# Three of eight weighted expert ranks added by TensorE through diagonals, in a two-block network on one core

## The chip, the core and the metric

The kernel runs on one core of one Trainium2 chip. A core has five engines that matter here: TensorE (matmuls into PSUM, the accumulators), VectorE, ScalarE, GpSimd (POOL in the profile) and SyncE (SP), whose queue only issues transfers. They meet through semaphores. The metric is the device time of one execution in microseconds (us), lower is better; the figure of a kernel is the median of its runs.

## What is computed

Two transformer-like blocks on 512 tokens of width 1024, in float32. The first block ends with a mixture of experts: every token picks 8 of 64 experts, each expert gives it one row of 1024 numbers, and the eight rows are weighted and added, together with a shared expert's output. Of the reference this is the part that matters:

```python
wts = jnp.take_along_axis(scores, top_e, axis=1)
wts = wts / jnp.sum(wts, axis=-1, keepdims=True) * ROUTED_SCALE
...
def expert_block(args):
    tok_b, w_b, e = args
    xb = h[tok_b]
    hid = jax.nn.silu(xb @ w_e_gate[e]) * (xb @ w_e_up[e])
    return (hid @ w_e_down[e]) * w_b[:, None].astype(h.dtype)
...
routed = jax.ops.segment_sum(out.reshape(n_pad, d), buf_tok, num_segments=n_tok)
shared = (jax.nn.silu(h @ w_sh_gate) * (h @ w_sh_up)) @ w_sh_down
return routed + shared
```

After it: `x = x + gt2 * rmsnorm(f_lat, g_post_ffn)`, then the second block.

## The kernel before

Everything of a width of 1024 is held feature-major: 8 tiles of 128 features by 512 tokens. The program is a list of stages (`phases`); each engine runs its function of a stage and all compute engines then meet (`meet`, L3059 to L3061). SP is outside of that: it has one stream of its own, which issues in program order, and a transfer that must wait holds everything behind it in the stream.

The experts' rows are unweighted when the expert stage (`moe_*`) writes them to `ys` in device memory, at row `k * T + token` for rank k (the k-th of a token's eight experts). The **gather stage** follows. Tokens go in four tiles of 128 (`TT` = 4), and for tile t and rank k one transfer (a gather, number n = 8t + k) brings 128 rows of 1024 numbers, 512 KB, into buffer `GB[k]`; there are eight buffers, so gather n goes where gather n - 8 was. In this stage

- SP issues the 32 gathers (L1817 to L1821), then the next chunks of the weight stream (`ring`, L3092), which the second block's first projection reads;
- VectorE (`gather_vector`) multiplies each arrived rank by its column of weights `W8[:, t, k]` and adds it up in `H2TOK[:, t, :]` (tokens by features), in the order of the ranks; each operation counts up `g_used`, and SP waits on that count before it refills a buffer;
- TensorE (`gather_tensor`) first puts the shared expert's second matmul into all eight PSUM banks (L2045), then, for each finished token tile, adds `H2TOK` on top: a matmul with the identity as moving operand turns tokens by features into features by tokens while it adds (L2050);
- ScalarE (`gather_scalar`) copies the eight banks out at the end (L2057).

The line by which SP holds a gather back:

```python
if n >= 8:
    sp.wait_ge(sem("g_used"), n - 7)
```

Behind the gather stage stand two norms (`norm`), each a chain ScalarE, VectorE, TensorE, ScalarE, VectorE, and then the projections of the second block (`dil_*`), where ScalarE takes the first weight chunk out of the ring at L259. DVE in the profile is VectorE, ACT is ScalarE. An f32 matmul leaves two records of a matmul and two of a weight load.

Of the kernel before, what the change touches and what calls it, by code (L numbers as in the profile page):

```python
# [16 lines left out]
ACT = mybir.ActivationFunctionType  # L17
# [7 lines left out]
P = 128  # L25
D = 1024
KT = D // P
# [3 lines left out]
TT = T // P  # L31
# [91 lines left out]
def two_blocks(nc, wstream, x_t, ctx_t, vecs, consts, rope_t, gmask_t, dmask_t, iota_t, w_dt, w_router,  # L123
               we_gu, we_down, w_z, w_gate_fb, h2, ys, x_saved, out_t, dbg, stop):
    ctx = ExitStack()
    with ctx:
# [5 lines left out]
        def sem(name):  # L132

            if name in MOE_SEMS:
                name = BLOCK1_SEMS[6 + MOE_SEMS.index(name)]
            if name in BLOCK2_SEMS:
                name = BLOCK1_SEMS[BLOCK2_SEMS.index(name)]
            if name not in made:
                made[name] = ctx.enter_context(nc.semaphore(name))
            return made[name]  # L140
# [26 lines left out]
        def bank(b, n=512, off=0):  # L167
            return pf[:, b * 512 + off:b * 512 + off + n]

        def view(at, *dims):  # L170
            n = 1
            for d in dims:
                n *= d
            ap = arena[:, at:at + n]
            if len(dims) == 2:
                return ap.rearrange("p (a b) -> p a b", b=dims[1])
            if len(dims) == 3:
                return ap.rearrange("p (a b c) -> p a b c", b=dims[1], c=dims[2])
            return ap
# [18 lines left out]
        C = {name: cst[:, i, :] for i, name in enumerate(CONSTS)}  # L198
        XT = view(0, KT, T)
        HT = view(4096, KT, T)  # L200
        R = 8192
# [24 lines left out]
        def arrived(pe, c):  # L226
            pe.wait_ge(sem(f"slot{c % NSLOT}_full"), 16 * (c // NSLOT + 1))
# [5 lines left out]
        def chunk_done(ins):  # L233
            ins.then_inc(sem("chunk_done"), 1)
# [1307 lines left out]
        H2TOK = view(R, TT, D)  # L1542
# [12 lines left out]
        W8 = view(K0, TT, 8)  # L1555
# [225 lines left out]
        def pairs(eng):  # L1781
            return eng.value_load(NPI[0:1, 0:1], min_val=T * 8 // P // 2, max_val=MAXBLK // 2)

        def moe_sync(sp):
            def load_gate_up(s, e):
                for j in range(2):
                    sp.dma_start(arena[:, EW[s][j]:EW[s][j] + CHW], we_gu[bass.ds(e * 2 + j, 1)].rearrange("o p n -> (o p) n")
                                 ).then_inc(sem(f"moe_w{s}{j}"), 16)

            def load_down(s, e):  # L1790
                sp.dma_start(arena[:, EW[s][2]:EW[s][2] + CHW], we_down[bass.ds(e, 1)].rearrange("o p n -> (o p) n")
                             ).then_inc(sem(f"moe_w{s}2"), 16)

            sp.wait_ge(sem("h2_tok"), 8)
            sp.dma_start(h2.rearrange("(t p) d -> p t d", p=P), H2TOK).then_inc(sem("h2_stored"), 16)
            sp.wait_ge(sem("rt_blocks"), 1)
            first = [sp.value_load(BEI[0:1, s:s + 1], min_val=0, max_val=E_N - 1) for s in range(2)]
            for s in range(2):
                load_gate_up(s, first[s])
            for s in range(2):  # L1800
                load_down(s, first[s])
            sp.wait_ge(sem("stage_ended"), 4 * MOE_STAGE)
            n = pairs(sp)
            with sp.Fori(1, n) as i:
                for s in range(2):
                    e = sp.value_load(BEI[0:1, bass.ds(i * 2 + s, 1)], min_val=0, max_val=E_N - 1)
                    for j in range(2):
                        sp.wait_ge(sem("moe_gu_used"), i * 4 + (2 * s + j + 1))
                        sp.dma_start(arena[:, EW[s][j]:EW[s][j] + CHW],
                                     we_gu[bass.ds(e * 2 + j, 1)].rearrange("o p n -> (o p) n")).then_inc(sem(f"moe_w{s}{j}"), 16)  # L1810
                for s in range(2):
                    e = sp.value_load(BEI[0:1, bass.ds(i * 2 + s, 1)], min_val=0, max_val=E_N - 1)
                    sp.wait_ge(sem("moe_d_used"), i * 2 + (s + 1))
                    load_down(s, e)
            for s in range(2):
                sp.wait_ge(sem(f"moe_out{s}"), n * 16 + 16)
            for n in range(32):  # L1817
                t, k = divmod(n, 8)
                if n >= 8:
                    sp.wait_ge(sem("g_used"), n - 7)  # L1820
                sp.dma_start(GB[n % 8], ys[k * T + t * P:k * T + t * P + P, :]).then_inc(sem(f"gathered{n % 8}"), 16)  # L1821

        def expert_hi(s, j):
# [202 lines left out]
        GB = [view(R + 6144 + 1024 * i, D) for i in range(8)]  # L2026
        F = view(R + 14336, KT, T)

        def gather_vector(dve):
            for n in range(32):  # L2030
                t, k = divmod(n, 8)
                dve.wait_ge(sem(f"gathered{n % 8}"), 16 * (n // 8 + 1))
                if k == 0:
                    dve.tensor_scalar(H2TOK[:, t, :], GB[n % 8], W8[:, t, 0:1], None, ALU.mult).then_inc(sem("g_used"), 1)
                else:
                    dve.wait_ge(sem("g_used"), n)
                    dve.scalar_tensor_tensor(H2TOK[:, t, :], GB[n % 8], W8[:, t, k:k + 1], H2TOK[:, t, :], ALU.mult,
                                             ALU.add).then_inc(sem("g_used"), 1)

        def gather_tensor(pe):  # L2040
            c = CH_SH + 2
            arrived(pe, c)
            for j in range(KT):
                for k in range(2):
                    pe.matmul(bank(j), ring[:, c % NSLOT, k * D + j * P:k * D + j * P + P], SHID[:, k, :],  # L2045
                              start=(k == 0), stop=(k == 1))
            for t in range(TT):
                pe.wait_ge(sem("g_used"), 8 * t + 8)
                for j in range(KT):
                    mm = pe.matmul(bank(j, P, t * P), H2TOK[:, t, j * P:j * P + P], C["ident"], start=False,  # L2050
                                   stop=(t == TT - 1), skip_group_check=True)
            chunk_done(mm)

        def gather_scalar(act):
            act.wait_ge(sem("chunk_done"), CH_SH + 3)
            for j in range(KT):
                act.activation(F[:, j, :], bank(j), ACT.Copy)  # L2057

        phases.append(dict(tensor=gather_tensor, scalar=gather_scalar, vector=gather_vector))
        norm(F, T, None, lambda k: gain[:, G2 + k:G2 + k + 1], residual=XT)  # L2060

# [1016 lines left out]
        def _(sp):  # L3078
            first_sync(sp)
            for c in range(CH_END if stop is None else LIMIT):  # L3080
                if c == CH_SH + 3:
                    moe_sync(sp)
                last = c - NSLOT
                if last in SPLIT and run_of(last) in LO_APART:
                    sp.wait_ge(sem("chunk_lo"), SPLIT.index(last) + 1)
                elif last >= 0:
                    sp.wait_ge(sem("chunk_done"), last + 1)
                if last == CH_DIL - 1:
                    sp.wait_ge(sem("semaphores_cleared"), 1)
                if last == CH_DIL:  # L3090
                    dil_swap(sp, 0)
                sp.dma_start(ring[:, c % NSLOT, :], wstream[c]).then_inc(sem(f"slot{c % NSLOT}_full"), 16)  # L3092
                if c == CH_ADA + NSLOT - 1:
                    tokens_sync(sp)
                if c == CH_QKV - 1:
                    tables_sync(sp)
                if CH_QKV <= last < CH_QKV + 8:
                    qk_swap(sp, last - CH_QKV)
                if CH_DIL <= last < CH_DIL + 35:
                    dil_swap(sp, 2 * (last - CH_DIL) + 1)  # L3100
                    dil_swap(sp, 2 * (last - CH_DIL) + 2)
# [29 lines left out]
def program(nc, a, out_t, dbg=None, stop=None):  # L3131
    h2 = nc.dram_tensor("h2", (T, D), F32, kind="Internal").ap()
    ys = nc.dram_tensor("ys", (8 * T + 1, D), F32, kind="Internal").ap()
    x_saved = nc.dram_tensor("x_saved", (P, KT, T), F32, kind="Internal").ap()
    two_blocks(nc, a["wstream"], a["x_t"], a["ctx_t"], a["vecs"], a["consts"], a["rope_t"], a["gmask_t"],
               a["dmask_t"], a["iota_t"], a["w_dt"], a["w_router"], a["we_gu"], a["we_down"], a["w_z"],
               a["w_gate_fb"], h2, ys, x_saved, out_t, dbg, stop)
# [129 lines left out]
```

## Time and profile before

| | us |
|---|---|
| median of 3 runs | 3883.09 |
| lowest, highest | 3882.57, 3893.02 |
| the profiled execution | 3883.08 |
| its span in the profile | 3881.3 |
| TensorE matmul busy in the span | 3554.1 (92%) |
| VectorE busy | 1576.2 (41%) |
| ScalarE busy | 1413.9 (36%) |

The span is what the hardware profiler recorded; what lies around it is start and end of the execution. The gather stage is a short stretch of it, from 1842.6 to 1897 us. A share of busy time over the whole span mixes all stages, so for one stage the timeline (instructions in order of time, neighbours of one line merged) and the windows (busy time in a given stretch) are the views to read. All times in the timeline count from the span's start.

### The profile page before, as it was taken

What the parts mean: (1) busy time and instruction counts of PE and PEld (TensorE: products, weight loads), DVE (VectorE), ACT (ScalarE), POOL (GpSimd) and SP (SyncE); (2) the same over time, 40 slices, a digit from 0 to 9 for tenths busy, and PEclk for the clock granted to TensorE, in tenths of its full rate; (3) what the DMA queues carried; (4) which work ended last, traced back from release to release, by engine and by line L of the source; (5) the groups of instructions that cost most, each with busy time, mean ns of one, the idle gap of its engine ahead of it and who ended that gap; (6) DMA issues with size and microseconds to landing.
All of it is one profiled execution on the core that took longest, in us unless ns stands there. A gap on an engine that the chain in (4) does not pass through costs nothing.

```text
span 3881.3 us, 44158 instructions
## 1 busy us (share of the span) xinstructions
PE 3554.1 (92%) x17320; PEld 2729.8 (70%) x17320; DVE 1576.2 (41%) x2226; ACT 1413.9 (36%) x1738; POOL 1189.7 (31%) x555
## 2 busy tenths in 40 slices
PE   7999897799869999999378999999999998899999
PEld 5975586578636766666257777776788877678887
DVE  4146525620266666665632333334421231243212
ACT  4135433342235555554133343443322232133221
POOL 3410123634202333332033323331344432124443
PEclk9999998899979999999589999999999997589999
DMA  5312110022229999997622221221222211013222
GB/s 217 94 66 88 64 56 22 1 76 98 87 95 335 354 349 355 368 367 287 238 65 87 71 74 60 74 71 49 88 98 98 98 55 55 1 55 109 98 98 76
DMA packets 94478, 494.53 MB, mean 127 GB/s; under 512 B 21646, under 2 KB 21902, under 8 KB 43760
## 3 DMA queue, kind: packets, MB, share of 16 engines
q1 hardware_dynamic: 74496, 452.75, 32.6%
q0 software_dynamic: 19824, 39.54, 2.8%
q8 instruction: 116, 1.90, 0.2%
q14 instruction: 42, 0.34, 0.0%
HBM read 470.18 MB, written 40.89 MB: 132 GB/s over the span
## 4 chain that ended last, share of the span: by engine, by line
PE 45%; DVE 2%; ACT 1%; issue 1%; POOL 1%; POOLq 0%; DMA 0%; ACTq 0%; DVEq 0%
PE ps L272 10%; PE ps L273 10%; PE ps L274 10%; PE ps L2219 2%; PE ps L2196 2%; PE ps L2174 1%; PE ps L2186 1%; PE ps L2207 1%; PE ps L2175 1%; PE ps L2176 1%; PE ps L2845 1%; PE ps L2832 1%; PE ps L2198 1%; PE ps L2840 0%; PE ps L280 0%
## 5 line engine op out<-in xcount | busy, mean ns | idle before, releaser
L272 PE MATMUL ps<-arena_r,arena_r 128*128 128x512 f32 x2080 | 844.1, 406 | 39.7 <-POOL ring_r L263 25.0
L273 PE MATMUL ps<-arena_r,arena_r 128*128 128x512 f32 x2080 | 817.7, 393 | 0.0
L263 POOL TENSOR_TENSOR ring_r<-ring,arena_r 128x2048 fp32r<-128x2048 f32 x100 | 466.2, 4663 | 887.7 <-ACT arena_r L259 887.7
L259 ACT ACTIVATE arena_r<-ring 128x2048 fp32r<-128x2048 f32 x166 | 316.7, 1909 | 564.0 <-PE ps L274 409.8
L272 PEld LDWEIGHTS ps<-arena_r,arena_r 128*128 128x128 f32 x2080 | 394.8, 190 | 144.7 <-issue 52.6
L273 PEld LDWEIGHTS ps<-arena_r,arena_r 128*128 128x128 f32 x2080 | 395.4, 190 | 88.5 <-issue 10.8
L263 POOL TENSOR_TENSOR arena_r<-ring,arena_r 128x2048 fp32r<-128x2048 f32 x66 | 303.9, 4605 | 414.4 <-ACT arena_r L259 414.4
L274 PE MATMUL ps<-arena_r,arena_r 128*128 128x512 f32 x1056 | 411.1, 389 | 0.0
L274 PE MATMUL ps<-arena_r,ring_r 128*128 128x512 f32 x1024 | 406.1, 397 | 0.0
L1949 DVE TENSOR_TENSOR arena_r<-arena,arena_r 128x2048 fp32r<-128x2048 f32 x132 | 301.8, 2288 | 165.2 <-ACT arena_r L1907 165.0
L1907 ACT ACTIVATE arena_r<-arena 128x2048 fp32r<-128x2048 f32 x132 | 250.8, 1910 | 124.6 <-DMA arena<-we_gu 101.3
L278 PE MATMUL ps<-arena_r,arena_r 128*128 128x256 f32 (+2 forms) x784 | 253.5, 323 | 15.5 <-DVE arena_r L300 15.5
L1861 PE MATMUL ps<-arena 128*128 128x512 f32 x528 | 240.7, 599 | 5.6 <-ACT arena L1924 5.1
L1846 PE MATMUL ps<-arena_r,arena_r 128*128 128x512 f32 x528 | 222.5, 421 | 5.2 <-DVE arena_r L1954 5.2
L274 PEld LDWEIGHTS ps<-arena_r,arena_r 128*128 128x128 f32 x1056 | 198.3, 188 | 41.1
L274 PEld LDWEIGHTS ps<-arena_r,ring_r 128*128 128x128 f32 x1024 | 196.6, 192 | 42.4
L1850 PE MATMUL ps<-arena_r,arena_r 128*128 128x512 f32 x528 | 207.0, 392 | 0.0
L1849 PE MATMUL ps<-arena_r,arena_r 128*128 128x512 f32 x528 | 206.5, 391 | 0.0
L2347 DVE CUSTOM_DVE_ANT_0 ps<-ps,arena 128x768 f32<-128x768 f32 x64 | 61.9, 967 | 298.8 <-PE ps L2198 298.8
L2600 DVE TENSOR_TENSOR arena<-ps,arena 128x512 f32<-128x512 f32 x44 | 30.4, 692 | 363.8 <-PE ps L274 363.8
L2313 POOL TENSOR_TENSOR arena<-arena,rope 128x512 f32<-128x512 f32 x48 | 62.0, 1291 | 373.3 <-DVE arena L2330 373.3
L278 PEld LDWEIGHTS ps<-arena_r,arena_r 128*128 128x128 f32 (+1 forms) x784 | 149.9, 191 | 28.7 <-issue 13.4
(388 smaller groups left out, 6101.1 us busy)
## 6 DMA issues: line engine op xcount, KB each, us to landing
ring<-wstream SPq DMA_DIRECT2D x193, 1024.0 KB, 4.9
arena<-we_gu SPq DMA_DIRECT2D x132, 1024.0 KB, 7.9
arena<-we_down SPq DMA_DIRECT2D x66, 1024.0 KB, 7.5
arena<-ys SPq DMA_DIRECT2D x32, 512.0 KB, 8.5
arena<-arena SPq DMA_DIRECT2D x192, 64.0 KB, 2.0
arena<-arena SPq DMA_DIRECT2D x32, 128.0 KB, 4.2
arena<-x_t SPq DMA_DIRECT2D x1, 2048.0 KB, 15.8
h<-arena SPq DMA_DIRECT2D x1, 2048.0 KB, 6.6
```

The source lines that it names most:

```text
L259: act.activation(whalf(c, 0), ring[:, c % NSLOT, :], ACT.Copy).then_inc(sem("chunk_hi"), 1)
L263: pool.tensor_tensor(whalf(c, 1), ring[:, c % NSLOT, :], whalf(c, 0).bitcast(F32), ALU.subtract).then_inc(sem("chunk_lo"), 1)
L272: pe.matmul(out, hi, rhs[0], start=start, stop=False)
L273: pe.matmul(out, hi, rhs[1], start=False, stop=False)
L274: return pe.matmul(out, lo, rhs[0], start=False, stop=stop)
L278: pe.matmul(out, a[0], b[0], start=start, stop=False)
L1846: mm = pe.matmul(bank(4 + s), x[0], hi[:, q * 512:q * 512 + 512], start=(k == 0), stop=False)
L1849: pe.matmul(bank(4 + s), x[0], lo[:, q * 512:q * 512 + 512], start=False, stop=False)
L1850: mm = pe.matmul(bank(4 + s), x[1], hi[:, q * 512:q * 512 + 512], start=False, stop=(k == KT - 1))
L1861: mm = pe.matmul(bank(2 * s + j), HIDT[s][:, k * P:k * P + P], expert_raw(s, 2)[:, k * D + j * 512:k * D + j * 512 + 512], start=(k == 0), ...
L1907: act.activation(expert_hi(s, j), expert_raw(s, j), ACT.Copy).then_inc(sem("moe_gu_hi"), 1)
L1949: dve.tensor_tensor(expert_lo(s, j), expert_raw(s, j), expert_hi(s, j).bitcast(F32), ALU.subtract).then_inc(sem("moe_gu_lo"), 1)
```

## The change

Ranks 0, 1 and 2 of a token are taken from VectorE. ScalarE first makes twelve diagonal matrices, `DIAG[:, t, k, :]` = identity times the weights of rank k in token tile t. TensorE then multiplies `GB[k]` (128 tokens by 128 features, as stationary operand) by this diagonal: that weights, turns and adds into PSUM in one matmul, eight matmuls for a rank of a token tile. VectorE keeps ranks 3 to 7 and starts its sum with rank 3. Buffers 0 to 2 are given back by TensorE (`g_turned`, the semaphore `st_sums` in use), buffers 3 to 7 by VectorE (`g_used`); `g_diag` is the semaphore `st_sq`.

```diff
@@ moe_sync
                 t, k = divmod(n, 8)
-                if n >= 8:
-                    sp.wait_ge(sem("g_used"), n - 7)
+                if t and k < NPE:
+                    sp.wait_ge(sem(g_turned), sums + NPE * (t - 1) + k + 1)
+                elif t:
+                    sp.wait_ge(sem("g_used"), (8 - NPE) * (t - 1) + k - NPE + 1)
                 sp.dma_start(GB[n % 8], ys[k * T + t * P:k * T + t * P + P, :]).then_inc(sem(f"gathered{n % 8}"), 16)
@@
+        NPE = 3
+        DIAG = view(R + 18432, TT, NPE, P)
+        g_diag, squares = "st_sq", 2 * KT
+        g_turned, sums = "st_sums", 2
+
         def gather_vector(dve):
-            for n in range(32):
-                t, k = divmod(n, 8)
-                dve.wait_ge(sem(f"gathered{n % 8}"), 16 * (n // 8 + 1))
-                if k == 0:
-                    dve.tensor_scalar(H2TOK[:, t, :], GB[n % 8], W8[:, t, 0:1], None, ALU.mult).then_inc(sem("g_used"), 1)
-                else:
-                    dve.wait_ge(sem("g_used"), n)
-                    dve.scalar_tensor_tensor(H2TOK[:, t, :], GB[n % 8], W8[:, t, k:k + 1], H2TOK[:, t, :], ALU.mult,
-                                             ALU.add).then_inc(sem("g_used"), 1)
+            for t in range(TT):
+                for k in range(NPE, 8):
+                    n = (8 - NPE) * t + k - NPE
+                    dve.wait_ge(sem(f"gathered{k}"), 16 * (t + 1))
+                    if k == NPE:
+                        dve.tensor_scalar(H2TOK[:, t, :], GB[k], W8[:, t, k:k + 1], None, ALU.mult).then_inc(sem("g_used"), 1)
+                    else:
+                        dve.wait_ge(sem("g_used"), n)
+                        dve.scalar_tensor_tensor(H2TOK[:, t, :], GB[k], W8[:, t, k:k + 1], H2TOK[:, t, :], ALU.mult,
+                                                 ALU.add).then_inc(sem("g_used"), 1)
@@ gather_tensor
             for t in range(TT):
-                pe.wait_ge(sem("g_used"), 8 * t + 8)
+                for k in range(NPE):
+                    pe.wait_ge(sem(g_diag), squares + NPE * t + k + 1)
+                    pe.wait_ge(sem(f"gathered{k}"), 16 * (t + 1))
+                    for j in range(KT):
+                        mm = pe.matmul(bank(j, P, t * P), GB[k][:, j * P:j * P + P], DIAG[:, t, k, :], start=False, stop=False,
+                                       skip_group_check=True)
+                    mm.then_inc(sem(g_turned), 1)
+                pe.wait_ge(sem("g_used"), (8 - NPE) * (t + 1))
                 for j in range(KT):
@@ gather_scalar
+            for t in range(TT):
+                for k in range(NPE):
+                    act.activation(DIAG[:, t, k, :], C["ident"], ACT.Copy, scale=W8[:, t, k:k + 1]).then_inc(sem(g_diag), 1)
             act.wait_ge(sem("chunk_done"), CH_SH + 3)
```

On TensorE, from the shared expert's matmul to the end of the first token tile, there stood before:

```order
L2045 MATMUL ps<-arena,ring 128x512 [waits slot1_full,stage_ended]
L2045 MATMUL ps<-arena,ring 128x512 x15
L2050 MATMUL ps<-cst,arena 128x128 [waits g_used]
L2050 MATMUL ps<-cst,arena 128x128 x7
```

and there stands now:

```order
L2053 MATMUL ps<-arena,ring 128x512 [waits slot1_full,stage_ended]
L2053 MATMUL ps<-arena,ring 128x512 x15
L2060 MATMUL ps<-arena 128x128 [waits gathered0,st_sq]
L2060 MATMUL ps<-arena 128x128 x7
L2060 MATMUL ps<-arena 128x128 [waits gathered1,st_sq]
L2060 MATMUL ps<-arena 128x128 x7
L2060 MATMUL ps<-arena 128x128 [waits gathered2,st_sq]
L2060 MATMUL ps<-arena 128x128 x7
L2065 MATMUL ps<-cst,arena 128x128 [waits g_used]
L2065 MATMUL ps<-cst,arena 128x128 x7
```

Three groups of eight matmuls stand between the shared expert's matmul and the adding of a tile, each behind a gather and a diagonal.

On SP, from the end of the expert loop to the next weight chunks, before:

```order
L1821 DMA arena<-ys 128x1024 [waits moe_out1,moe_out0]
L1821 DMA arena<-ys 128x1024 x7
L1821 DMA arena<-ys 128x1024 [waits g_used] x24
L3092 DMA ring<-wstream 128x2048 [waits chunk_done] x2
```

and now:

```order
L1823 DMA arena<-ys 128x1024 [waits moe_out1,moe_out0]
L1823 DMA arena<-ys 128x1024 x7
L1823 DMA arena<-ys 128x1024 [waits st_sums] x3
L1823 DMA arena<-ys 128x1024 [waits g_used] x5
```

The last two rows come three times, once for each token tile behind the first, and then the weight chunks. The number and order of the gathers are the same; nine of the 24 that wait now wait for TensorE's groups (`st_sums`) in place of VectorE.

## Rows read from the trace of the kernel before

**Rows 1.** The page: the span, and busy time, share and instructions of two engines.

```profile
span 3881.3 us, 44158 instructions
PE 3554.1 (92%) x17320; PEld 2729.8 (70%) x17320; DVE 1576.2 (41%) x2226; ACT 1413.9 (36%) x1738; POOL 1189.7 (31%) x555
```

**Rows 2.** Timeline of VectorE: start, us, engine, line, operation, count, [idle before <- releaser].

```profile
1846.35 0.75 DVE L2034 TENSOR_SCALAR arena<-arena 128x1024 f32<-128x1024 f32 x1 [8.29 <-DMA arena<-ys]
1847.55 1.28 DVE L2037 SCALAR_TENSOR_TENSOR arena<-arena 128x1024 f32<-128x1024 f32 x1 [0.45 <-DMA arena<-ys]
1849.69 8.23 DVE L2037 SCALAR_TENSOR_TENSOR arena<-arena 128x1024 f32<-128x1024 f32 x6 [0.85 <-DMA arena<-ys]
1857.84 0.75 DVE L2034 TENSOR_SCALAR arena<-arena 128x1024 f32<-128x1024 f32 x1
1858.69 9.62 DVE L2037 SCALAR_TENSOR_TENSOR arena<-arena 128x1024 f32<-128x1024 f32 x7
...
1879.46 9.61 DVE L2037 SCALAR_TENSOR_TENSOR arena<-arena 128x1024 f32<-128x1024 f32 x7
```

**Rows 3.** Timeline of TensorE's matmuls, from the expert stage's end to the gather stage's.

```profile
1833.47 3.17 PE L1861 MATMUL ps<-arena 128*128 128x512 f32 x7
1843.46 17.01 PE L2045 MATMUL ps<-arena,ring 128*128 128x512 f32 x32 [6.83 <-POOLq L3060]
1860.31 1.95 PE L2050 MATMUL ps<-cst,arena 128*128 128x128 f32 x16
1868.36 3.78 PE L2050 MATMUL ps<-cst,arena 128*128 128x128 f32 x16 [6.11 <-DVE arena L2037]
1878.75 3.78 PE L2050 MATMUL ps<-cst,arena 128*128 128x128 f32 x16 [6.60 <-DVE arena L2037]
1889.13 3.78 PE L2050 MATMUL ps<-cst,arena 128*128 128x128 f32 x16 [6.60 <-DVE arena L2037]
```

**Rows 4.** Timeline of ScalarE at the stage's end.

```profile
1893.01 4.03 ACT L2057 ACTIVATE arena<-ps 128x512 f32<-128x512 f32 x8 [58.57 <-PEq L3060]
1897.12 1.28 ACT L238 ACT_TABLE_LOAD   x1
```

**Rows 5.** Timeline of SP's issues; then the gathers' line: issue to landing.

```profile
1842.61 36.43 SPq L1821 DMA_DIRECT2D arena<-ys  x32
1879.09 0.91 SPq L3092 DMA_DIRECT2D ring<-wstream  x2
...
DMA to landing us min/median/max: 3.6/8.5/10.1
```

**Rows 6.** Windows: busy us of five engines, then granted clock, DMA share, GB/s.

```profile
1838.00:1840.00 2.00, 0.00 (x0) 0.00 (x0) 0.06 (x1) 0.00 (x0) 0.84 (x2) 0.83 0.09 37
1848.00:1850.00 2.00, 2.00 (x4) 0.76 (x3) 1.15 (x2) 0.00 (x0) 0.00 (x0) 0.61 1.00 395
1860.00:1862.00 2.00, 2.00 (x18) 1.76 (x16) 1.82 (x2) 0.00 (x0) 0.00 (x0) 1.00 1.03 410
1866.00:1868.00 2.00, 0.00 (x0) 0.00 (x0) 1.90 (x2) 0.00 (x0) 0.00 (x0) 0.65 1.03 410
1872.00:1874.00 2.00, 0.15 (x1) 0.00 (x0) 1.90 (x2) 0.00 (x0) 0.00 (x0) 0.50 1.03 410
```

**Rows 7.** The second block: a burst of transposes on TensorE, and windows over it.

```profile
3333.64 3.78 PE L2809 MATMUL ps<-cst,arena 128*128 128x128 f32 x16 [1.11 <-ACT arena L2913]
...
3336.00:3338.00 2.00, 1.42 (x7) 1.13 (x6) 1.15 (x3) 1.32 (x4) 0.62 (x1) 0.56 0.00 0
3338.00:3340.00 2.00, 0.00 (x0) 0.00 (x0) 1.14 (x2) 1.99 (x5) 2.00 (x2) 1.00 0.00 0
```

**Rows 8.** Groups by line and shape: ScalarE's small copies; busy us, mean ns, idle.

```profile
L1924 ACT ACTIVATE arena<-ps 128x256 f32<-128x256 f32 x33 | 12.4, 376 | 0.0
```

**Rows 9.** Timeline of ScalarE: the second block takes its first weight chunks.

```profile
1953.38 3.71 ACT L259 ACTIVATE arena_r<-ring 128x2048 fp32r<-128x2048 f32 x2 [0.81 <-DVEq L3060]
```

## The prediction

> **What bounds the kernel now.** The totals [rows 1] say TensorE is busy for 92% of the span and VectorE for 41%, but that mean says nothing about this stage, so I went to the timeline of the gather stage, engine by engine, and then to the transfers. VectorE [rows 2] starts rank 0 of the first token tile at 1846.35 us, idles twice for the second and third arrival, and from 1849.69 on runs without a gap: a token tile takes 0.85 us for its first rank (1857.84 to 1858.69) and 9.62 / 7 = 1.37 us for each of the seven others, 10.4 us in all, until 1889.07. TensorE [rows 3] multiplies the shared expert's second weight from 1843.46 to 1860.31, which no gather needs, then adds a token tile (8 matmuls, two records each) whenever VectorE has finished one; it waits 6.1 to 6.6 us before each of the last three, and its last burst ends at 1892.91 (1889.13 + 3.78). ScalarE's copies follow at once [rows 4], and after them the norm, a plain chain. So the end of TensorE's last burst is the figure that matters; what shifts it shifts all that follows.
>
> The transfers decide as much. The window view [rows 6] has the DMA engines at a share of 1.03 and 410 GB/s in the middle of the stage. One gather is 512 KB, 1.28 us at that rate; eight are 10.2 us, against VectorE's 10.4. **The two are level**: VectorE is the bound by 0.15 us a tile and the transfers stand right behind it. A gather lands 8.5 us after its issue in the median, 3.6 at least [rows 5]; the first one was issued at 1842.61 and used at 1846.35, 3.74 us, which I take for a gather that finds the engines idle.
>
> **What the change removes.** Three ranks of each of four token tiles leave VectorE: a tile costs it 0.85 + 4 x 1.37 = 6.3 us in place of 10.4, 16.5 us less in all. With the transfers at 10.2 us a tile, that alone can buy almost nothing: the 32nd gather could not land before 1846.35 + 31 x 1.28 = 1886.0, VectorE would end at 1887.4 and TensorE at 1891.2, a gain of 1.7 us.
>
> **What it adds.** ScalarE makes 12 diagonals of 128x128; the nearest row is a 128x256 copy of 376 ns [rows 8], so at most 12 x 0.38 = 4.5 us, from about 1842 on, under TensorE's shared matmuls: nothing on the path, and TensorE's wait for them costs nothing. TensorE gets 12 groups of 8 matmuls of exactly the shape of its present adding (128x128 f32, two records each): 1.95 us at 2.4 GHz (the burst at 1860.31) or 3.78 us at 1.2 GHz (that at 1868.36) [rows 3]. In a tile it then has four groups, 7.8 or 15.1 us. By count this is free or not according to the clock, since the transfers take 10.2 us.
>
> **What it moves, and where the loss is.** Buffers 0 to 2 are now freed by TensorE, which gets to them only behind the shared matmuls. SP issues in order: gather 8 (tile 1, rank 0) waits for TensorE's first group, and the 23 gathers behind it, five of them into buffers that VectorE empties early, stand in the same queue. Before, gather 8 could go once the first VectorE operation ended at 1847.1. Now:
>
> Tile 0. The shared matmuls end at 1860.31; the three groups end at 1862.3, 1864.2 and 1866.2 (granted clock 1.00 there [rows 6]), the adding at 1868.1. Gathers 8, 9, 10 are issued at 1862.3, 1864.2, 1866.2 and land 3.7 us later, 1866.0, 1867.9, 1869.9; gathers 11 to 15 follow, 1.28 us apart, the last at 1876.3. The DMA engines, busy throughout before, stand nearly empty from 1855.3 (the eighth arrival, 1846.35 + 7 x 1.28) to about 1864. VectorE now starts with rank 3, so with the fourth arrival, no later than 1851, and is done with the tile at about 1857; nothing waits for that.
>
> Tile 1. TensorE's three groups run 1868.1 to 1874.0. VectorE's last rank lands at 1876.3 and is done at 1877.7. TensorE idles 3.7 us. The clock had fallen after the last matmul records of the expert stage ended at 1836.64 (granted 0.83 of full speed on average over 1838 to 1840) and again in the idle time behind 1862.3 (0.65 over 1866 to 1868) [rows 3, 6]; I take it to fall here, so the adding costs 3.78: 1881.5.
>
> Tile 2. TensorE now has work without a pause. When it last began at 1.2 GHz with unbroken work, at 1843.46, 2.4 GHz came at about 1849.6 (0.61 over 1848 to 1850), 6.1 us later; here that is 1883.8. The three groups end at 1884.6, 1886.5, 1888.5. Gathers 16 to 23 stream at the full rate, behind gather 15, until 1886.5, VectorE is done at 1887.9, and the adding ends at 1890.4.
>
> Tile 3. Gathers 24 to 26 are issued at 1884.6, 1886.5, 1888.5, so SP holds the last five until 1888.5, a second hold. They land from 1893.5 to 1898.6, VectorE ends at 1900.0; TensorE, done with its groups at 1896.3, idles 3.7 us and adds at 1.2 GHz until 1903.8.
>
> That is 1903.8 - 1892.9 = **10.9 us later**. The profiled execution took 3883.08 us (its span 3881.3 and 1.8 around it), within 0.01 of the median of the three runs, so the forecast is 3883.1 + 10.9 = **3894.0 us**, 0.28% more. The stages behind do not take it up: SP issues the next weight chunks about 12 us later than at 1879.09 [rows 5], but ScalarE first reads them at 1953.38 [rows 9].
>
> Price bounds. Low: a group is never under 1.95. High: after a pause the first arrivals may be slower than 1.28 apart; the third use of the stage came 2.14 us after the second [rows 2], 0.8 more than the pace, and with two restarts that is +1.6. The burst that brings the clock back would now be of 128-column matmuls, not of the 512-column ones of 1843: 16 such records from 3333.64 on, all at 1.2 GHz, ended with a granted clock of 0.56 over 3336 to 3338 and 1.00 after [rows 7], so these also lift it, which is why I take the return.
>
> What a page says against this change: the Trainium skill, "TensorE: Matmul & The Clock Gate", section "HAM oscillation — how this bites in real kernels", has matmul bursts that are shorter than the wait for their data fall back to the low clock once for every burst. By that rule the trace agrees: the three waits of 6.1 to 6.6 us were each followed by a burst at 1.2 GHz. Were every group behind 1877.7 cold, as that rule would have it if the waits go on, the sum would be the first rival's below. The same skill, "DMA: Bandwidth & Descriptors", section "Where 436 GB/s comes from", puts the ceiling at about 435 GB/s and says HBM binds at some 358; this trace holds 410, above the second. At 435 a gather would take 1.20 us, an estimate from that page, and the sum, with ten arrivals on its path, would be 0.8 us lower.
>
> **Rivals.** (a) *The clock does not come back.* From 1877.7 TensorE has nine groups left, 9 x 3.78 = 34.0 us, all data early: 1911.7, 18.8 us later, 3901.9 us. For it: before, this stage kept 1.2 GHz from 1868 to its end. Against: there it was idle most of the time, and rows 7. It decides if the granted clock stays at 0.50 through 1885. (b) *The clock never falls.* For it: the pause of 3.7 us is shorter than those before the three last bursts [rows 3]. Adding ends at 1879.7, the groups of tile 2 at 1885.5, gather 31 lands at 1896.8, VectorE ends at 1898.1, TensorE at 1900.1 to 1901.9: 7.2 to 9.0 us later, 3890.3 to 3892.1. Against it: the fall behind 1836.64, which by the 0.83 over 1838 to 1840 came at 1839.3, 2.7 us behind the last matmul [rows 3, 6]. (c) *The other side: not slower.* If the gathers were not held back (the transfers' 10.2 us a tile the only bound), TensorE's last burst would end at 1891.2, or at 1889.3 if warm: 3879.5 to 3881.4. It holds if buffer 0 is free by 1851.6, 3.7 us ahead of the eighth arrival; the order on TensorE puts that at 1862.3. (d) *Dearer hand-overs.* TensorE to SP to DMA to VectorE is passed twice on the path; with slow restarts, or a group of diagonals dearer than the adding, 12.5 to 15 us later, 3895.6 to 3898.
>
> **How the numbers follow.** Main case 0.60, 3891.5 to 3896.0; (a) 0.15; (b) 0.08; (c) 0.06; (d) 0.09; something unseen 0.02. A measurement of this kernel tells about 0.3%, 11.7 us, from no change; the main case lies just inside that line, with three quarters of its weight: within 0.3%: 0.45 + 0.08 + 0.05 = 0.58. Slower by more: 0.15 + 0.15 + 0.09 = 0.39. Faster by more: 0.03; the transfers exclude it. The range takes in (b), (d) and (a) and leaves (c) out: 3887 to 3903.
>
> **What would show it.** In the changed profile: a hole of some 9 us in the DMA share behind about 1855; gather 8 issued at 1862.3; SP's longest waits on TensorE's groups, not on VectorE; VectorE idle for about 14 us between tile 0 and tile 1 (1857 to 1871); TensorE's last burst at about 1900 to 1904; everything behind it shifted alike. Wrong would be: gathers 8 to 15 issued before 1860 (then (c)); a granted clock of 1.00 at 1880 (then (b)) or 0.50 at 1890 (then (a)); a group that is not 1.95 or 3.78 us.

## The result

The changed kernel took 3903.9 us in the median of 6 runs (3899.28 to 3911.24), the kernel before 3885.24 us in 6 runs beside them (3882.32 to 3893.02): a ratio of 1.0048, 95% interval 1.0034 to 1.0061. It is slower, and by more than the 3894.0 us forecast; 3903.9 also lies outside of the range of 3887 to 3903. Over all experiments the kernel before was run 120 times on several chips, with 3877.22 to 3903.87 us and a median of 3888.04: the executions of one program scatter by 0.3% downwards and 0.4% upwards.

The profiled execution of the changed kernel took 3906.59 us:

```profile
span 3904.7 us, 44541 instructions
PE 3578.2 (92%) x17512; PEld 2751.4 (70%) x17512; DVE 1560.5 (40%) x2214; ACT 1416.6 (36%) x1750; POOL 1189.9 (30%) x555
```

Against [rows 1] VectorE has 15.7 us less work and TensorE 24 us more, as the edit says; neither tells where 23 us came from. TensorE's timeline of the gather stage, which answers [rows 3] (start, us, engine, line, operation, count, idle time before and its releaser):

```profile
1853.18 17.02 PE L2053 MATMUL ps<-arena,ring 128*128 128x512 f32 x32 [6.83 <-POOLq L3078]
1870.04 5.52 PE L2060 MATMUL ps<-arena 128*128 128x128 f32 x48
1875.40 1.95 PE L2065 MATMUL ps<-cst,arena 128*128 128x128 f32 x16
1877.19 5.52 PE L2060 MATMUL ps<-arena 128*128 128x128 f32 x48
1889.64 3.78 PE L2065 MATMUL ps<-cst,arena 128*128 128x128 f32 x16 [6.93 <-DVE arena L2045]
1893.22 5.63 PE L2060 MATMUL ps<-arena 128*128 128x128 f32 x48
1899.89 2.05 PE L2065 MATMUL ps<-cst,arena 128*128 128x128 f32 x16 [1.04 <-DVE arena L2045]
1901.78 5.52 PE L2060 MATMUL ps<-arena 128*128 128x128 f32 x48
1912.66 3.78 PE L2065 MATMUL ps<-cst,arena 128*128 128x128 f32 x16 [5.37 <-DVE arena L2045]
```

L2060 are the groups of ranks 0 to 2 (three groups in a row), L2065 the adding of VectorE's sum. I measure **the stage** from the start of the shared matmuls (L2053, before L2045) to the end of TensorE's last burst: 1912.66 + 3.78 - 1853.18 = 63.3 us, and before 1889.13 + 3.78 - 1843.46 = 49.5 us. So 13.8 us of the loss are here. The other 9.7 us of this one execution had come before the stage began (1853.18 against 1843.46), in work that the change doesn't touch. ScalarE's copies and all behind them are shifted alike: from their start to the span's end it is 1988.2 us here (they start at 1916.48) and 1988.3 before [rows 4].

VectorE's timeline, for [rows 2]:

```profile
1859.93 0.75 DVE L2042 TENSOR_SCALAR arena<-arena 128x1024 f32<-128x1024 f32 x1 [12.16 <-DMA arena<-ys]
1861.11 5.45 DVE L2045 SCALAR_TENSOR_TENSOR arena<-arena 128x1024 f32<-128x1024 f32 x4 [0.43 <-DMA arena<-ys]
1881.31 0.75 DVE L2042 TENSOR_SCALAR arena<-arena 128x1024 f32<-128x1024 f32 x1 [14.75 <-DMA arena<-ys]
1884.14 5.45 DVE L2045 SCALAR_TENSOR_TENSOR arena<-arena 128x1024 f32<-128x1024 f32 x4 [2.07 <-DMA arena<-ys]
...
1905.86 0.75 DVE L2042 TENSOR_SCALAR arena<-arena 128x1024 f32<-128x1024 f32 x1 [6.03 <-DMA arena<-ys]
1907.16 5.45 DVE L2045 SCALAR_TENSOR_TENSOR arena<-arena 128x1024 f32<-128x1024 f32 x4 [0.54 <-DMA arena<-ys]
```

It idles ahead of every tile for a gather, 14.75 us between tiles 0 and 1. What SP waited for (us in total, times, longest), and then windows over the hole in the transfers and over the restart (busy us of five engines, granted clock, DMA share, GB/s), for [rows 5, 6]:

```profile
SPq L1823 <- PE ps L2060: 29.9, 9, 15.5
SPq L1823 <- DVE arena L2045: 5.2, 5, 1.9
```

```profile
1862.00:1864.00 2.00, 2.00 (x6) 0.84 (x5) 1.79 (x3) 0.00 (x0) 0.00 (x0) 1.00 0.95 383
1864.00:1866.00 2.00, 2.00 (x6) 0.95 (x5) 1.90 (x2) 0.00 (x0) 0.00 (x0) 1.00 0.05 20
...
1870.00:1872.00 2.00, 2.00 (x19) 1.96 (x18) 0.00 (x0) 0.00 (x0) 0.00 (x0) 1.00 0.00 0
1872.00:1874.00 2.00, 2.00 (x20) 2.00 (x20) 0.00 (x0) 0.00 (x0) 0.00 (x0) 1.00 0.50 145
1874.00:1876.00 2.00, 2.00 (x20) 2.00 (x20) 0.00 (x0) 0.00 (x0) 0.00 (x0) 1.00 0.80 242
1876.00:1878.00 2.00, 2.00 (x21) 2.00 (x20) 0.00 (x0) 0.00 (x0) 0.00 (x0) 1.00 0.77 227
1878.00:1880.00 2.00, 2.00 (x21) 2.00 (x20) 0.00 (x0) 0.00 (x0) 0.00 (x0) 1.00 0.98 363
1880.00:1882.00 2.00, 2.00 (x21) 2.00 (x20) 0.69 (x1) 0.00 (x0) 0.00 (x0) 1.00 1.03 412
...
1894.00:1896.00 2.00, 2.00 (x20) 2.00 (x19) 1.51 (x2) 0.00 (x0) 0.00 (x0) 1.00 0.82 328
1896.00:1898.00 2.00, 2.00 (x20) 2.00 (x19) 1.90 (x2) 0.00 (x0) 0.00 (x0) 1.00 0.84 268
1898.00:1900.00 2.00, 0.96 (x9) 0.77 (x8) 1.73 (x2) 0.00 (x0) 0.00 (x0) 1.00 0.79 248
```

SP stood for 15.5 us behind TensorE's first group, and the DMA engines moved nothing from 1866 to 1872. When the gathers started again they ran at 227 to 242 GB/s for 4 us and at 363 for 2 more before 412 came back; around the second restart (gather 24, issued at 1895.30, 5.7 us behind gather 23) it was 248 to 373 GB/s from 1894 to 1906. The forecast had arrivals at the full pace there, but for the three behind TensorE's groups.

### The profile page after: what moved, and what is told of

Same layout as the page of the kernel before. It is cut to its first block and busy times, and to the rows that moved or that the text cites. A ratio compares the mean times of both kernels' runs of the same rounds, so it can differ in the third digit from the quotient of the medians.

```text
span 3904.7 us, 44541 instructions
## 1 busy us (share of the span) xinstructions
PE 3578.2 (92%) x17512; PEld 2751.4 (70%) x17512; DVE 1560.5 (40%) x2214; ACT 1416.6 (36%) x1750; POOL 1189.9 (30%) x555
## 5 line engine op out<-in xcount | busy, mean ns | idle before, releaser
L272 PEld LDWEIGHTS ps<-arena_r,arena_r 128*128 128x128 f32 x2080 | 395.1, 190 | 145.8 <-issue 52.4
L1909 ACT ACTIVATE arena_r<-arena 128x2048 fp32r<-128x2048 f32 x132 | 250.4, 1910 | 131.4 <-DMA arena<-we_gu 108.7
L1863 PEld LDWEIGHTS ps<-arena 128*128 128x128 f32 x528 | 95.0, 190 | 113.0 <-issue 106.1
```

The source lines that it names most:

```text
L272: pe.matmul(out, hi, rhs[0], start=start, stop=False)
L1863: mm = pe.matmul(bank(2 * s + j), HIDT[s][:, k * P:k * P + P], expert_raw(s, 2)[:, k * D + j * 512:k * D + j * 512 + 512], start=(k == 0), ...
L1909: act.activation(expert_hi(s, j), expert_raw(s, j), ACT.Copy).then_inc(sem("moe_gu_hi"), 1)
```

## The experiments

My theory was that the loss is SP's in-order queue standing behind TensorE, so transfers that are lost, and not the work that TensorE got. The rivals were TensorE's added matmuls and their clock, and something outside of the stage.

**The hold alone.** The kernel before, plus a wait of SP for the end of the shared matmuls:

```diff
+                if n == 8:
+                    sp.wait_ge(sem("st_sums"), 3)
                 if n >= 8:
                     sp.wait_ge(sem("g_used"), n - 7)
@@ gather_tensor, behind the shared matmuls
+            mm.then_inc(sem("st_sums"), 1)
```

> The kernel before, all eight ranks on VectorE, with one thing added: SP may issue gather 8 only when TensorE's shared matmuls are done. The stage is measured from the start of the shared matmuls to the end of TensorE's last burst: 49.45 us before, 63.26 us changed. Theory of the hold (SP's in-order queue behind TensorE costs transfers, and no other wait matters here): gathers 8 to 15 are issued from 17.1 us behind the start of the shared matmuls, land from 20.8 us on, VectorE ends tile 1 some 10.5 to 11.5 us later, so 6.5 to 8 us longer than before, stage 56 to 57.5 us, and no second hold. Rival (TensorE's added matmuls and their clock are what costs, the transfers have room): less than 2 us longer, stage below 51.5 us. Of the whole time the first expects 6 to 8 us more than before, ratio 1.0015 to 1.002.

Ratio 1.0016 (1.0004 to 1.0029). TensorE and VectorE in its timeline:

```profile
1851.37 15.64 PE L2047 MATMUL ps<-arena,ring 128*128 128x512 f32 x32 [6.83 <-POOLq L3063]
...
1902.46 3.68 PE L2053 MATMUL ps<-cst,arena 128*128 128x128 f32 x16 [6.63 <-DVE arena L2039]
...
1870.74 0.75 DVE L2036 TENSOR_SCALAR arena<-arena 128x1024 f32<-128x1024 f32 x1 [5.71 <-DMA arena<-ys]
```

The stage is 54.8 us, 5.3 over the one before, a little under the 56 to 57.5 expected: the clock rose earlier in this execution, so the shared matmuls ended 15.5 us behind their start and not 16.85, and so did the hold. VectorE waits 5.7 us ahead of tile 1 and 0.5 behind its first rank, and then never again. A wait on SP costs this much with no work moved at all; 54.8 us is well clear of the rival's 51.5.

**The diagonals alone.** The kernel before with ScalarE's twelve activations and nobody who reads them.

```diff
+            for t in range(TT):
+                for k in range(3):
+                    act.activation(DIAG[:, t, k, :], C["ident"], ACT.Copy, scale=W8[:, t, k:k + 1]).then_inc(sem("st_sq"), 1)
```

> The kernel before with the twelve diagonals made by ScalarE in the gather stage and used by nobody. The changed kernel's median lies 18.7 us above the one before, while its stage is only 13.8 us longer; in its profile the rest came ahead of the gather stage (2.3 us before the expert loop, 7.4 us in it). Theory A (that rest is scatter between executions of the same instructions): stage 49.45 us within 0.3, total ratio 1.000 within 0.001. Rival B (added instructions, or the code behind them that they push along, slow the expert loop or take time in the stage): 3 to 8 us more, ratio 1.001 to 1.002, the loop's iterations longer than 20.5 us on average.

Ratio 1.0002 (0.999 to 1.0013), stage 49.7 us (1844.72 to 1894.41). The twelve take 3.6 us of ScalarE and nothing of the stage. Theory A.

**No hold.** The changed kernel with a second set of three buffers, taken by the odd token tiles:

```diff
-                if t and k < NPE:
-                    sp.wait_ge(sem(g_turned), sums + NPE * (t - 1) + k + 1)
-                elif t:
+                if t > 1 and k < NPE:
+                    sp.wait_ge(sem(g_turned), sums + NPE * (t - 2) + k + 1)
+                elif t and k >= NPE:
                     sp.wait_ge(sem("g_used"), (8 - NPE) * (t - 1) + k - NPE + 1)
+        GX = [GB[:3], [view(R + 20480 + 1024 * i, D) for i in range(3)]]
```

> The changed kernel with a second set of buffers for ranks 0 to 2 (odd token tiles go into the second set), so SP waits for TensorE's groups of two tiles back and never in the shared matmuls. Nothing else differs. Theory of the hold: the transfers run without a hole, gather 31 lands about 42.5 us behind the start of the shared matmuls, VectorE ends at 44 to 45, TensorE's last burst at 46.5 to 49: stage 47 to 49.5 us, 14 to 16 us under the changed kernel, level with the kernel before or up to 2 us under it. Rival (TensorE's added matmuls are the bound, at 1.2 GHz or by their number): stage 58 us or more, only 3 to 5 us under the changed kernel.

Ratio 0.9999 (0.9986 to 1.0012). TensorE:

```profile
1842.91 16.22 PE L2059 MATMUL ps<-arena,ring 128*128 128x512 f32 x32 [6.83 <-POOLq L3084]
...
1880.58 5.52 PE L2066 MATMUL ps<-arena 128*128 128x128 f32 x48
1888.92 3.39 PE L2071 MATMUL ps<-cst,arena 128*128 128x128 f32 x16 [2.83 <-DVE arena L2051]
```

The stage is 1892.31 - 1842.91 = 49.4 us. The same work on the same engines as in the changed kernel, and all of the 13.8 us are gone: **the loss is the hold, in full**. Nor is there a gain: the transfers are as long as VectorE's work was, and the last adding still waited 2.83 us for VectorE and took 3.39 us, most of it at 1.2 GHz.

**The last ranks in place of the first.** TensorE takes ranks 5 to 7, so that in tile 1 only three gathers, and not eight, stand behind it (the constants in `moe_sync`, `gather_vector`, `gather_tensor` and `gather_scalar` change to match):

```diff
-                if t and k < NPE:
+                if t and k >= 8 - NPE:
```

> The changed kernel with the last three ranks (5 to 7) on TensorE in place of the first three: SP's order of gathers is the same, but of tile 1 only the last three now stand behind TensorE. Theory of the hold: gathers 8 to 12 go out while the shared matmuls run, 13 to 15 at 18.9, 20.7 and 22.5 us behind their start, the hole in the transfers shrinks from about 9 us to about 3, no further hold; stage 51 to 56 us. Rival (the cost is TensorE's added work): as the changed kernel, 62 to 64 us.

Ratio 1.0006 (0.9994 to 1.0018). The first row and the last:

```profile
1842.75 16.10 PE L2053 MATMUL ps<-arena,ring 128*128 128x512 f32 x32 [6.83 <-POOLq L3078]
...
1893.22 1.95 PE L2065 MATMUL ps<-cst,arena 128*128 128x128 f32 x16
```

The stage is 1895.17 - 1842.75 = 52.4 us, inside the theory's 51 to 56.

**The changed kernel again,** for the part of the loss outside of the stage.

> The changed kernel once more. Its first median was 18.7 us over the one before, but its stage (start of the shared matmuls to the end of TensorE's last burst) only 13.8 us longer. If the rest is scatter of the expert stage ahead of it, this median lies 11 to 16 us over the kernel before (ratio 1.003 to 1.004) and the stage is again 62.5 to 64 us. If the changed program slows something outside of the stage, it is again 17 us or more (ratio over 1.0043) with the same stage.

3902.56 us against 3889.05: 13.5 us, ratio 1.0040 (1.0023 to 1.0057). Its first and its last burst:

```profile
1845.48 15.86 PE L2053 MATMUL ps<-arena,ring 128*128 128x512 f32 x32 [6.83 <-POOLq L3078]
...
1904.71 3.78 PE L2065 MATMUL ps<-cst,arena 128*128 128x128 f32 x16 [5.90 <-DVE arena L2045]
```

The stage is 63.0 us again. It begins at 1845.48 here and at 1853.18 in the first profile, of the same program: 7.7 us of scatter ahead of the stage, 4.8 of them in the expert loop. In the eleven profiles of the other experiments it begins between 1839.7 and 1851.4.

**TensorE kept at work.** The changed kernel with matmuls that add zeros in its two long pauses (tiles 1 and 3), so that the clock has no cause to fall:

```diff
+                for j in range((0, 28, 0, 22)[t]):
+                    pe.matmul(bank(j % 8, P, t * P), C["ident"], ZERO, start=False, stop=False, skip_group_check=True)
                 pe.wait_ge(sem("g_used"), (8 - NPE) * (t + 1))
```

> The changed kernel with matmuls that add zeros on TensorE in its two long pauses, 28 in tile 1 and 22 in tile 3, so that it has work until VectorE's sum is ready. If the clock falls in those pauses and this costs, the adding of tiles 1 and 3 takes 1.95 us in place of 3.78 each, the gathers of tile 3 are released 1.8 us earlier, and the stage is 59 to 60.5 us in place of 63.3. If the clock has no part in the loss, the stage stays at 62.5 us or more.

```profile
1875.09 2.05 PE L2068 MATMUL ps<-cst,arena 128*128 128x128 f32 x16 [0.37 <-DVE arena L2046]
...
1885.32 3.63 PE L2068 MATMUL ps<-cst,arena 128*128 128x128 f32 x16 [2.81 <-DVE arena L2046]
...
1899.06 1.95 PE L2068 MATMUL ps<-cst,arena 128*128 128x128 f32 x16
```

Stage 1901.01 - 1839.70 = 61.3 us; ratio to before 1.0027 (1.0014 to 1.0041). The adding of tiles 1 and 3 did take 2.05 and 1.95 us, but TensorE then came to tile 2 earlier than VectorE's sum, waited 2.81 us, and did that adding cold. So the stage is 2.0 us shorter, less than the 2.8 to 4.3 expected. Part of even that is scatter, since the shared matmuls ended 16.1 us behind their start here and 16.9 in the first profile: counted from their end it is 45.2 us, against 46.4 in the first profile and 47.3 in the repeat. These cold addings are a small part of the loss, 1.2 to 2.1 us.

**The first hold or the later ones.** Second set of buffers, but the waits for tiles 2 and 3 as in the changed kernel:

```diff
-                    sp.wait_ge(sem(g_turned), sums + NPE * (t - 2) + k + 1)
+                    sp.wait_ge(sem(g_turned), sums + NPE * (t - 1) + k + 1)
```

> The kernel with the second set of buffers, but for tiles 2 and 3 SP still waits for TensorE's groups of the tile just before, as in the changed kernel; only the first hold, behind the shared matmuls, is gone. If the later holds and the restarts behind them cost too, the stage is 51.5 to 55 us (49.4 with no hold, 63.3 with all). If the first hold is all, it is 49.5 to 50.5 us.

```profile
1841.35 15.68 PE L2059 MATMUL ps<-arena,ring 128*128 128x512 f32 x32 [6.83 <-POOLq L3084]
...
1893.55 2.05 PE L2071 MATMUL ps<-cst,arena 128*128 128x128 f32 x16
```

Stage 54.25 us, inside the 51.5 to 55 for holds that cost too; ratio 1.0007 (0.9993 to 1.002). Without the hold at gather 8 the stage is 63.3 - 54.25 = 9.0 us shorter, and 54.25 - 49.4 = 4.9 us over the kernel without any hold are left. These are not the costs of the changed kernel's first and later holds, though. SP's waits here:

```profile
SPq L1824 <- PE ps L2066: 14.6, 5, 9.8
```

The wait of 9.8 us is at gather 16, which went out at 1866.00, behind TensorE's first group of tile 1; in the changed kernel gather 16 followed gather 15 by 1.05 us (1878.12, 1879.17), and the second long hold was at gather 24. Taking the first hold away let SP run into the next one. What each hold of the changed kernel costs by itself stays open.

**Better than both?** Second set of buffers and the last ranks together:

> Second set of buffers and the last three ranks on TensorE: no hold, and what arrives last in the last tile is taken by TensorE's groups, 1.79 us each, not by VectorE's operations with a burst behind. With the transfers as the only bound the 32nd gather lands about 43 us behind the start of the shared matmuls, its group ends at 45, the adding at 47: stage 45 to 47.5 us, 2 to 4.5 us under the kernel before; of the whole time a ratio of 0.999 to 0.9995, which five rounds hardly tell from 1. If TensorE or the clock is the bound, 49 us or more.

Ratio 1.0002 (0.9991 to 1.0013), stage 1898.63 - 1847.65 = 51.0 us: a miss by 3.5 us or more. I put it on the two weight chunks of 1 MB that SP issues while the last gathers are under way, and held them back:

```diff
+            for x in range(NPE):
+                sp.wait_ge(sem(landed(3, x)), 48)
```

> The kernel with both changes (second set of buffers, last three ranks on TensorE), whose stage came out at 51.0 us where 45 to 47.5 was expected, with one more: SP issues the two weight chunks of 1 MB only when the last three gathers have landed. There the chunks were issued at 1881.1, while TensorE still waited for gathers until 1889.6, and the transfers ran at 410 GB/s throughout. If the chunks take bandwidth from the last gathers, the last group now ends 3 to 5 us earlier and the stage is 46 to 48 us. If the gathers in flight land in order ahead of them, nothing moves: 50.5 to 51.5.

Ratio 0.9998 (0.9986 to 1.0009). First the last two bursts without, then with this wait:

```profile
1889.62 7.22 PE L2067 MATMUL ps<-arena 128*128 128x128 f32 x48 [2.86 <-DMA arena<-ys]
1896.68 1.95 PE L2072 MATMUL ps<-cst,arena 128*128 128x128 f32 x16
```

```profile
1886.61 5.60 PE L2069 MATMUL ps<-arena 128*128 128x128 f32 x48 [2.86 <-DMA arena<-ys]
1892.04 1.95 PE L2074 MATMUL ps<-cst,arena 128*128 128x128 f32 x16
```

The stage is 49.1 us with the wait, again outside of what I expected. And it is not the chunks: the gather for which TensorE waits came 42.0 us behind the start of the shared matmuls without the wait (1889.62 - 1847.65) and 41.7 with it (1886.61 - 1844.87). What differs are the three groups, 7.22 against 5.60 us: after the same pause of 2.86 us the granted clock fell in the one execution (0.67 over 1890 to 1892, then 0.50) and stayed at 1.00 in the other. The kernel before with the chunks held back likewise:

> The kernel before with the same later issue of the two weight chunks. VectorE runs without a gap to the end there, so earlier landings cannot help: stage 49.2 to 49.9 us, ratio 1.000. A stage of 48 us or less would say that the chunks also hold back the kernel before.

Ratio 0.9988 (0.9975 to 1.0), stage 49.0 us (1848.84 to 1897.80), 0.2 under the range because the three last addings took 3.4 to 3.6 us; its VectorE runs without a gap as before. It is not told from no change.

**Fewer gathers in flight.** After the kernel with late chunks I believed that the last three gathers had landed together, since TensorE's three groups ran back to back:

```diff
+                if n >= 4:
+                    u, i = divmod(n - 4, 8)
+                    sp.wait_ge(sem(landed(u, i - 5) if i >= 5 else f"gathered{i}"), 16 * (u // 2 + 1 + u % 2 if i >= 5 else u + 1))
```

> The last kernel (second buffers, last ranks on TensorE, weight chunks later) with at most four gathers in flight: SP waits for the landing of gather n - 4 before it issues gather n. There the DMA engines were done at about 1887.2, and TensorE's three last groups ran one after the other from 1886.6: the last three gathers had landed together. If gathers in flight share the engines and so land in a bunch, with four in flight the landings come one by one, 1.28 us apart, at the same 400 to 410 GB/s; the first of the last three groups starts 2 to 3 us earlier and the stage is 46.5 to 47.5 us in place of 49.1. If the bunching has another cause, 48.8 us or more; if four do not fill the engines (below 380 GB/s), 51 us or more.

```profile
1882.00 5.60 PE L2072 MATMUL ps<-arena 128*128 128x128 f32 x48 [2.79 <-DMA arena<-ys]
1887.43 1.95 PE L2077 MATMUL ps<-cst,arena 128*128 128x128 f32 x16
```

Ratio 0.9999 (0.9988 to 1.0011), stage 1889.38 - 1840.14 = 49.2 us: that reading was false. Here SP issued the weight chunks, so saw the last gather landed, at 1884.49, 2.5 us behind the landing at 1882.00, with one gather between: 1.25 us apart. In the kernel with late chunks the same two times are 1886.61 and 1889.13, 2.5 us. They had never been bunched. Three groups of 1.79 us are slower than three landings, so this design ends at the landing of gather 29 plus 5.4 plus 1.95: 41.8 + 7.4 = 49.2 us. With the landings at this pace that is its floor, and it is where the kernel before stands.

The changed kernel with at most three in flight:

```diff
+                if n >= 3:
+                    sp.wait_ge(sem(f"gathered{(n - 3) % 8}"), 16 * ((n - 3) // 8 + 1))
```

> The changed kernel with at most three gathers in flight, all else as it was, holds and all. In it gather 11 landed 5.4 us after its issue and VectorE had to wait 2 us more for gather 12, with everything there after that. If that bunching made the stage 2.9 us longer than the 60.3 which the forecast's arrivals, 1.28 us apart, gave, VectorE's last operation in tile 1 now ends 1 to 2.5 us earlier, measured from the start of the shared matmuls (36.5 before), and the stage is 59 to 62 us. If not, 63 us or more, and longer if three do not fill the engines.

Ratio 1.0051 (1.0037 to 1.0065), stage 67.5 us (1845.62 to 1913.15), and VectorE's last operation of tile 1 ended 36.6 us behind the start, no earlier; counted from the end of the shared matmuls it is 20.3 us here and 19.6 in the changed kernel, so later. Windows of 4 us, first of this kernel, then of the one with four in flight:

```profile
1872.00:1876.00 4.00, 2.78 (x23) 2.42 (x22) 1.26 (x2) 0.00 (x0) 0.00 (x0) 1.00 0.84 277
1876.00:1880.00 4.00, 0.00 (x0) 0.00 (x0) 2.62 (x3) 0.00 (x0) 0.00 (x0) 0.73 0.96 288
1880.00:1884.00 4.00, 1.74 (x8) 1.74 (x9) 2.01 (x2) 0.00 (x0) 0.00 (x0) 0.50 0.99 313
```

```profile
1856.00:1860.00 4.00, 4.00 (x38) 4.00 (x38) 3.69 (x4) 0.00 (x0) 0.00 (x0) 1.00 1.03 418
```

With three gathers in flight the engines moved about 290 GB/s behind the hold, at a share of 0.84 to 0.99 (one window ahead of the hold, 1848 to 1852, has 379), with four up to 418. That a cap of three is slow is shown by the stage of 67.5 us. It fits the low rate right behind a hold, where TensorE frees one buffer every 1.79 us until the five buffers of VectorE join.

The low rate does not by itself explain how late VectorE was in tile 1, however. In the changed kernel's first profile, from the issue of gather 8 to the moment at which VectorE gets gather 12:

```profile
1872.02:1884.14 12.12, 10.69 (x96) 10.50 (x95) 0.76 (x2) 0.00 (x0) 0.00 (x0) 1.00 0.85 300
```

That is 3.6 MB, nearly seven gathers, while gather 12 is only the fifth: later gathers had been moved in part before it was complete. Gathers 8 to 12 took 3.1, 3.5, 4.2, 5.3 and 7.7 us from issue to landing, and gather 12 landed 2.8 us behind gather 11, in one jump. In the repeat of the same program the jump comes one gather later, ahead of gather 13:

```profile
1873.89 1.29 DVE L2045 SCALAR_TENSOR_TENSOR arena<-arena 128x1024 f32<-128x1024 f32 x1 [0.50 <-DMA arena<-ys]
1876.73 4.07 DVE L2045 SCALAR_TENSOR_TENSOR arena<-arena 128x1024 f32<-128x1024 f32 x3 [1.55 <-DMA arena<-ys]
```

Such a jump comes without a hold too: in the kernel with the second buffers and the last ranks gather 20 landed 2.4 us behind gather 19, in the middle of transfers at 400 GB/s. What makes it no run shows. Behind the second hold the low rate does fit: gathers 24 to 27 landed 2.0 to 2.3 us apart, while the rate was 248 to 268 GB/s.

## Why the prediction was wrong, step by step

- **What bounds the kernel**: right. Taking 16 us from VectorE won nothing; with every hold removed the stage was 49.4 us, level with before. The predicted gain without a hold, 1.7 us, was not there either: 49.4 us against 49.45.
- **ScalarE's diagonals**: right, 3.6 us under the shared matmuls (at most 4.5 said), and no cost in the run with them alone.
- **TensorE's groups**: shape right, 1.79 us each in a row (5.36 for three, 1870.04 to 1875.40) where 1.95 was taken.
- **The first hold**: right in kind, place and start. Gather 8 was issued 18.84 us behind the start of the shared matmuls (1872.02 - 1853.18), as the steps had it (1862.3 - 1843.46), VectorE idled 14.75 us (about 14 said), the DMA engines stood empty. That the holds together are the loss is shown; how it divides among them is not.
- **The step that failed: the arrival of the gathers behind a hold.** The mechanism was right and this term of the sum too small. I took 3.7 us from issue for gathers 8 to 10, 24 to 26, and then 1.28 us from one to the next, from stretches with eight in flight. Behind the first hold gather 11 landed 9.3 us behind the issue of gather 8 where the steps put 8.9, and gather 12 12.1 where they put 10.2: 0.4 us of slow restart and one jump that is 1.5 us over the pace. Behind the second hold VectorE got gather 27 10.6 us behind the issue of gather 24 (1905.86 - 1895.30) where they put 8.9. VectorE's last operation of tile 1 ended 36.4 us behind the start of the shared matmuls (1889.59 - 1853.18) where the steps put 34.2 (1877.7 - 1843.5), and that of tile 3 59.4 (1912.61 - 1853.18) where they put 56.5. This is the whole of 63.3 - 60.3: the sum said 10.9 us, the stage shows 13.8. The price bound of +1.6 for it was from the start of the stage, with eight issued at once; rival (d) had 12.5 to 15, with a chance of only 0.09. Why one gather in such a row lands 2.8 us behind the one before stays open.
- **The clock**: right for tile 1 (3.78 us after a pause of 6.93) and tile 3 (3.78 after 5.37). It came back 3.8 us after TensorE's restart at 1889.64 (0.64 over 1892 to 1894), not 6.1, which gave some of the loss back. Rival (a), whose 3901.9 us lies nearest to the measured time, did not happen: TensorE was at 2.4 GHz from 1894 until the pause ahead of the last adding (0.62 over 1910 to 1912). That agreement of numbers is chance.
- **The page rule on bursts** (the Trainium skill, "TensorE: Matmul & The Clock Gate", section "HAM oscillation — how this bites in real kernels") holds in kind: the long pauses did cool the adding. It does not carry the result: keeping TensorE busy in them gave back 1.2 to 2.1 us.
- **The rest, from 13.8 to 18.7 us**: scatter, by all that the runs show. The measured 3903.9 lies 9.9 us over the forecast: 2.1 are the base (3885.2 in place of 3883.1), 2.9 the step above, 4.9 came outside of the stage. With the step mended and nothing else the forecast would have been 3883.1 + 13.8 = 3896.9, inside of the range, so it is the scatter that put the median 0.9 us beyond 3903. It came ahead of the stage in the profile, the repeat had 13.5 us with the same stage, and the added instructions alone did nothing. My forecast took one execution that agreed with a median of three within 0.01 us as if the base were that sharp; the range had no term for it, though the three runs shown reached 3893.02. With the scatter of 0.3% in it, and the main case where it belonged, it would have reached beyond 3903.
- **The chances**: the main case was put "just inside" the 0.3% line with 0.45 of 0.60. A mechanism whose missing terms (slow restarts, hand-overs) all point one way should not have its weight on the near side of a line.

## What to carry to other kernels

When work moves to another engine, its buffers are given back by that engine too: look at what else stands in that engine's queue, and at everything behind the waiting transfer in the queue that issues. Here 17 us of matmuls that no gather needed held 24 gathers, and three more buffers undid the whole loss. And where transfers and an engine are level, relieving the engine buys nothing, while a hole in the transfers is paid for: 5.3 us for one wait of SP with no work moved, 13.8 for the holds of the changed kernel with what came late behind them.

## What the hardware showed beyond what I expected

- 512 KB gathers from one queue: at most three in flight moved 277 to 337 GB/s in windows of 4 us behind the restart, four 368 to 418, eight 410 in a steady stretch. The DMA share of busy time was already 0.84 to 0.99 with three: a high share is no proof of full speed.
- Gathers of one queue do not each land when their share of the bytes has been moved: 3.6 MB had been moved behind the first hold when the fifth gather of 512 KB became usable.
- After a pause of 2.8 to 2.9 us TensorE's clock fell in some executions and not in others (7.22 against 5.60 us for the same three groups).
- One program on one core scattered by 27 us over 120 executions (3877.22 to 3903.87), more than the effect under study; the length of the stage in a profile repeated within 0.3 us (63.3 and 63.0), though the shared matmuls in it took 16.9 and 15.7 us by when the clock rose.
